# Convolution filters made in pieces inside the first feed-forward stage, their spectra kept in HBM and loaded into x's place; feed-forward blocks of 6, 6, 5 and 5 tiles

## The reference, cut to what matters

```python
def encoder_layer(x, lp):
    x = x + 0.5 * swiglu(rms_norm(x, lp['norm_ffn1']), lp['ffn1_w_in'], lp['ffn1_w_out'])
    h = rms_norm(x, lp['norm_mix'])
    pa, pb, pc = jnp.split(h @ lp['w_in'], [A_COLS, A_COLS + B_COLS], axis=-1)
    ya = rwkv7_mixer(pa, lp)
    yb = group_rms_norm(neighbourhood_attention(pb, lp['na_rpb']), lp['na_out_norm'], B_HEADS)
    yc = group_rms_norm(hyena_mixer(pc, lp), lp['hy_out_norm'], C_GROUPS)
    x = x + jnp.concatenate([ya, yb, yc], axis=-1) @ lp['w_out']
    return x + 0.5 * swiglu(rms_norm(x, lp['norm_ffn2']), lp['ffn2_w_in'], lp['ffn2_w_out'])

def hyena_filters(seq_len, lp):          # from weights and positions alone, never from x
    h = jnp.sin(freq * (z @ w1 + b1)); h = jnp.sin(freq * (h @ w2 + b2))
    h = (h @ w3).reshape(seq_len, 2, HY_ORDER, C_DIM) * jnp.exp(-t * jnp.abs(deltas))
    kern = concatenate([h_fwd, zeros, flip(h_bwd[1:])])
    return kern / jnp.sum(jnp.abs(kern), axis=0)

def hyena_mixer(p, lp):
    v, x1, x2 = jnp.split(short_conv(p), 3, axis=-1)
    kern_fft = jnp.fft.rfft(hyena_filters(seq_len, lp), axis=0)
    z = x1 * (fft_long_conv(v, kern_fft[:, 0]) + v * d_skip[0])
    return x2 * (fft_long_conv(z, kern_fft[:, 1]) + z * d_skip[1])
```

## Time and profile before

| what | value |
|---|---|
| median of 3 runs | 3818.8 us (3816.16 to 3823.51) |
| the profiled execution's own time | 3818.56 us |
| its span | 3816.8 us |
| PE busy | 3555.1 us (93%) |
| PEld busy | 3311.8 us (87%) |
| DVE busy | 1745.3 us (46%) |
| ACT busy | 951.7 us (25%) |
| POOL busy | 33.9 us (1%) |
| chain that ended last, share of PE | 88% |
| mean granted TensorE clock | 0.966 of full |

### The profile page before, as it was taken

How to read it: one execution, slowest core, us unless ns; L and a number is a source line. 1 busy time by engine, 2 the same in 40 slices (tenths; PEclk the granted TensorE clock), 3 DMA queues, 4 the chain that set the end, 5 groups by cost and what they waited for, 6 DMA issues and landing times.

```text
span 3816.8 us, 59772 instructions
## 1 busy us (share of the span) xinstructions
PE 3555.1 (93%) x26416; PEld 3311.8 (87%) x26416; DVE 1745.3 (46%) x2916; ACT 951.7 (25%) x1479; POOL 33.9 (1%) x32
## 2 busy tenths in 40 slices
PE   7999999999858799999999999999998668999997
PEld 7999998878734699999999999988886348999997
DVE  4333346536565543333443333464466564433333
ACT  3212132223251322121321121311233413212121
POOL 0000000000000000000000000000000010000000
PEclk9999999999977899999999999999998789999999
DMA  3111212310230112211112211223004101211211
GB/s 113 64 65 61 66 56 98 107 48 3 84 149 0 39 61 67 70 62 61 61 63 65 67 61 60 96 68 120 16 3 167 66 1 56 67 61 61 67 63 54
DMA packets 67841, 249.67 MB, mean 65 GB/s; under 512 B 7424, under 2 KB 7424, under 8 KB 66176
## 3 DMA queue, kind: packets, MB, share of 16 engines
q1 hardware_dynamic: 67584, 245.85, 19.2%
HBM read 222.23 MB, written 23.59 MB: 64 GB/s over the span
## 4 chain that ended last, share of the span: by engine, by line
PE 88%; DVE 7%; ACT 2%; issue 1%; DMA 1%; POOL 0%; SPq 0%; DVEq 0%; POOLq 0%; ACTq 0%
PE ps L635 87%; DVE uv L1951 1%; PE ps L1067 1%; DVE rstd L1523 0%; DMA hdecay<-hyc 0%; ACT sqb L1167 0%; DMA x<-xT 0%; PE ps L988 0%; DVE hl L1531 0%; DVE NR L1693 0%; DVE sc L2002 0%; ACT sqb L1171 0%; DVE mixed L1882 0%; DVE yab L1959 0%; DVE ml L2027 0%
## 5 line engine op out<-in xcount | busy, mean ns | idle before, releaser
L635 PE MATMUL ps<-hh,wh 128*128 128x384 f32 (+2 forms) x3520 | 1181.2, 336 | 24.6 <-DVE wl L1513 23.6
L635 PE MATMUL ps<-hl,wh 128*128 128x384 f32 (+2 forms) x3520 | 1178.4, 335 | 0.0
L635 PE MATMUL ps<-hh,wl 128*128 128x384 f32 (+2 forms) x3520 | 1177.9, 335 | 0.0
L635 PEld LDWEIGHTS ps<-hh,wh 128*128 128x128 f32 x3520 | 662.8, 188 | 41.2 <-issue 24.2
L635 PEld LDWEIGHTS ps<-hl,wh 128*128 128x128 f32 x3520 | 662.7, 188 | 14.6
L635 PEld LDWEIGHTS ps<-hh,wl 128*128 128x128 f32 x3520 | 662.6, 188 | 14.1
L1190 ACT CAST wh<-wring 128x1024 fp32r<-128x1024 f32 (+1 forms) x340 | 339.7, 1026 | 658.1 <-PE ps L635 653.3
L635 PE MATMUL ps<-act_high,wl 128*128 128x384 f32 x1408 | 470.3, 334 | 0.0
L635 PE MATMUL ps<-act_high,wh 128*128 128x384 f32 x1408 | 470.3, 334 | 0.0
L635 PE MATMUL ps<-act_low,wh 128*128 128x384 f32 x1408 | 470.3, 334 | 0.0
L1574 DVE TENSOR_TENSOR silu<-ps,rstd 128x384 f32<-128x384 f32 x176 | 98.1, 557 | 730.1 <-PE ps L635 730.1
(11 more groups left out here) (260 smaller groups left out, 3440.2 us busy)
## 6 DMA issues: line engine op xcount, KB each, us to landing
wring<-wa SPq DMA_DIRECT2D x308, 512.0 KB, 3.6
wring<-wa SPq DMA_DIRECT2D x32, 384.0 KB, 3.1
bias<-bias SPq DMA_DIRECT2D x24, 512.0 KB, 7.9
conv_q_k<-stage SPq DMA_DIRECT2D x28, 384.0 KB, 2.6
outT<-x SPq DMA_DIRECT2D x2, 3072.0 KB, 9.8
x<-outT SPq DMA_DIRECT2D x2, 3072.0 KB, 25.8
conv<-conv_q_k SPq DMA_DIRECT2D x2, 2304.0 KB, 20.6
vwin<-v_rows SPq DMA_DIRECT2D x14, 256.0 KB, 13.7
```

Source lines behind the costliest of these rows:

```text
L635: return pe.matmul(out, lhsT, rhs, start=start, stop=stop)
```

## The change

`FF_BLOCKS` becomes 6, 6, 5 and 5 tiles, in both feed-forward stages, which frees room behind the activations for the filters' buffers. `filters` leaves the mixer. In the first feed-forward stage each engine calls a `filters` of its own after each unit, and the table `FILTER_AT` says which units are followed by a job: 2 for the network, 6 for taps (two tiles of positions each, one order, 256 columns for each direction), 4 sums, 6 folds. GpSimd adds the magnitudes into `acc` before TensorE sums them over the partitions; the norm is now applied to the spectrum itself, in `kst`, which GpSimd stores to HBM (`kern_rows`), six pieces of 512 KB a layer. GpSimd also loads the filters' inputs and tables. In the mixer SP loads the whole spectrum into x's place and x after the last product of the second convolution; `ftab` and `gtab` are loaded behind bias 4. The transposes of the convolution alternate with the four group norms; v and x1 are copied together, even tiles by VectorE, odd ones by ScalarE.

```diff
-FF_BLOCKS = [(0, 8), (8, 8), (16, 6)]
+FF_BLOCKS = [(0, 6), (6, 6), (12, 5), (17, 5)]
+FF_MOST = max(n for _, n in FF_BLOCKS)
+FF_OUTS = 2 * OUT_TILES * len(FF_BLOCKS)
...
+TAP_TILES = [(0, 1, 2, 3), (4, 5)]
+SEG_FOLDS = [(0, 1), (2,)]
+TAP_GROUPS = [(0, 0), (1, 0), (0, 1), (1, 1)]
+KERNEL_STORES = [(o, a) for o, s in TAP_GROUPS for a in SEG_FOLDS[s]]
+FILTER_AT = {2: ("mlp", 1), 5: ("mlp", 2), 7: ("taps", 0, 0, 0), 8: ("taps", 0, 0, 2), 9: ("sum", 0, 0),
+             13: ("kern", 0, 0), 14: ("kern", 0, 1), 15: ("taps", 1, 0, 0), 16: ("taps", 1, 0, 2), 18: ("sum", 1, 0),
+             20: ("kern", 1, 0), 21: ("kern", 1, 1), 25: ("taps", 0, 1, 4), 27: ("sum", 0, 1), 29: ("kern", 0, 2),
+             35: ("taps", 1, 1, 4), 37: ("sum", 1, 1), 39: ("kern", 1, 2)}
+FILTER_LAST_IN = [("nrm", 0, 0), ("kern", 1, 1), ("kern", 0, 2), ("kern", 1, 2)]
...
+        sums = hy1("sums", [P, 3, 2, 512])
+        odd = hy1("odd", [P, 2, 512])
+        kern = nc.alloc_sbuf_tensor_at("kern", [P, 3, 2, 2, 512], F32, offset=16544)
...
                 sp.dma_start(conv[:, :, :], cqk[l, 0:C_TILES].rearrange("n p t -> p n t")).then_inc(s_cl, 16)
-                sp.wait_ge(s_spill, 16 * (l + 1))
-                sp.dma_start(x[:, :, :], outT).then_inc(s_back, 16)
+                sp.wait_ge(s_kst, 96 * (l + 1))
+                sp.dma_start(kern[:, :, :, :, :].rearrange("p a k t c -> p a (k t c)"),
+                             kern_d[l].rearrange("a p k c -> p a (k c)")).then_inc(s_kl, 16)
+                sp.wait_ge(*rv.at(l, "done", 1))
                 for k in range(BIASES, QUADS):
                     load_bias(k)
-                sp.wait_ge(s_g4, 6 * l + 4)
...
+                    if k == BIASES:
+                        for t, n in ((ftab[:, :, :, :].rearrange("p a b c -> p (a b c)"), "forward"),
+                                     (gtab[:, :, :].rearrange("p a b -> p (a b)"), "inverse")):
+                            sp.dma_start(t, hy_d[:, HOFF[n]:HOFF[n] + dict(HCOLS)[n]]).then_inc(s_hy, 16)
+                sp.wait_ge(s_spill, 16 * (l + 1))
+                sp.wait_ge(*hv.at(l, "dft", 1, FOLD_ORDER[-1]))
+                sp.dma_start(x[:, :, :], outT).then_inc(s_back, 16)
...
+            def filter_taps(l, n):
+                o, s = TAP_GROUPS[n]
+                for p in TAP_TILES[s]:
+                    pool.wait_ge(*fa.at(l, "abs", o, p))
+                    if p == TAP_TILES[s][0]:
...
+                        m = pool.tensor_copy(acc[:, :], taps[:, p % 2, :])
+                    else:
+                        pool.wait_ge(*fg.at(l, "acc", o, p - 1))
+                        m = pool.tensor_tensor(acc[:, :], acc[:, :], taps[:, p % 2, :], ALU.add)
+                    m.then_inc(*fg.inc(l, "acc", o, p))
...
+            def store_kernel(l, n):
+                o, s = TAP_GROUPS[n]
+                for a in SEG_FOLDS[s]:
+                    pool.wait_ge(*fv.at(l, "scaled", o, a))
+                    pool.dma_start(kern_d[l, a][:, :, 256 * o:256 * o + 256], kst[:, :, :]).then_inc(s_kst, 16)
...
+                pool.wait_ge(s_gu, 4 * l * FT + 1)
+                pool.dma_start(w12[0:64, :], hw_d[l, 0:64, 0:HWOFF["w3"]]).then_inc(s_hz, 16)
...
+                load_decay(0)
+                load_table(0)
+                for n in range(len(TAP_GROUPS)):
+                    filter_taps(l, n)
+                    store_kernel(l, n)
+                    if n == 1:
+                        pool.wait_ge(*fv.at(l, "eo", 1, 3))
+                        load_decay(1)
+                        pool.wait_ge(*fp.at(l, "kern", 1, 0))
+                        load_table(2)
...
+            def filters(l, unit, block):
...
+                if block:
+                    pe.wait_ge(s_xup, x_count(l, 0) + 16 * block)
+                if job[0] == "mlp":
...
+                elif job[0] == "taps":
+                    _, o, s, p0 = job
+                    pe.wait_ge(*fa.at(l, "sin", 2))
...
+                    for p in (p0, p0 + 1):
+                        for dr in range(2):
+                            lo = 512 * dr + 256 * o
+                            m = mm(ps[:, 4 + p % 2, 256 * dr:256 * dr + 256], h1[0:64, fold_tokens(p)], hwt[0:64, lo:lo + 256])
+                        m.then_inc(*fp.inc(l, "taps", o, p))
+                elif job[0] == "sum":
+                    _, o, s = job
+                    pe.wait_ge(*fg.at(l, "acc", o, TAP_TILES[s][-1]))
...
+                    for dr in range(2):
+                        m = mm(bank(6, 256), cs("ones"), acc[:, 256 * dr:256 * dr + 256], dr == 0, dr == 1)
+                    m.then_inc(*fp.inc(l, "sum", o, s))
+                else:
+                    _, o, a = job
+                    s, even, odd_ = FOLDS[a]
+                    loads = {0: (2 * l + 1), 1: (2 * l + 1 + o), 2: (2 * l + 2)}[a]
+                    pe.wait_ge(s_tab[a % 2], 16 * loads)
+                    pe.wait_ge(*fv.at(l, "eo", o, TAP_TILES[s][-1]))
+                    if a == 1:
+                        pe.wait_ge(*fv.at(l, "kern", o, 0))
+                    for b, tiles in ((4, even), (5, odd_)):
+                        for trig, src in enumerate((se, so)):
+                            last = (b, trig) == (4, 0)
+                            for g in tiles:
+                                i = g - TAP_TILES[s][0]
+                                m = mm(ps[:, b, 256 * trig:256 * trig + 256], tables[a % 2][:, trig, i, :], src[:, i, :],
+                                       g == tiles[0], g == tiles[-1] and not last)
+                            if last:
+                                pe.wait_ge(*fv.at(l, "skip", o, s))
+                                m = mm(bank(4, 256), cs("ones", SKIP_ROW, SKIP_ROW + 1), skip_sum[SKIP_ROW:SKIP_ROW + 1, 0:256],
+                                       False, True)
+                    m.then_inc(*fp.inc(l, "kern", o, a))
...
+                            if f == 0:
+                                filters(l, 2 * j + hf_, b)
+                    if f == 0:
+                        pe.wait_ge(*fv.at(l, *FILTER_LAST_IN[b]))
...
             def hyena(l):
                 for g in range(6):
                     if g >= 2:
-                        pe.wait_ge(*hv.at(l, "tr", g - 2))
+                        pe.wait_ge(*(ha if g % 2 else hv).at(l, "tr", g - 2))
                     for j in range(4):
                         m = pe.transpose(ps[:, 4 + g % 2, P * j:P * j + P], conv[:, j, fold_tokens(g)], cs("ident"))
                     m.then_inc(*hp.inc(l, "tr", g))
...
+                    if g >= 2:
+                        gnorm()
                 for o in range(2):
                     if o == 0:
-                        pe.wait_ge(*hv.at(l, "tr", 5))
-                    src = vt if o == 0 else zt
+                        pe.wait_ge(*hv.at(l, "tr", 4))
+                        pe.wait_ge(*ha.at(l, "tr", 5))
+                        pe.wait_ge(s_hy, 32 * (l + 1))
+                        pe.wait_ge(s_g3, 6 * l + 4)
+                    src = (lambda g: vx[:, g, 0, :]) if o == 0 else (lambda g: zt[:, g, :])
...
+            def hyena(l):
+                for g in range(6):
+                    if g >= 2:
+                        gn(g)
+                    if g % 2:
+                        sa.wait_ge(*hp.at(l, "tr", g))
+                        sa.copy(vx[:, g, :, :].rearrange("p a c -> p (a c)"), bank(5)).then_inc(*ha.inc(l, "tr", g))
+                    if g >= 3:
+                        gn_root(6 * l + g - 3)
+                gn_root(6 * l + 3)
...
+                if job and job[0] == "taps":
+                    _, o, s, p0 = job
...
+                    for p in (p0, p0 + 1):
+                        ve.wait_ge(*fp.at(l, "taps", o, p))
+                        if p - 2 >= g0:
+                            ve.wait_ge(*fg.at(l, "acc", o, p - 2))
+                        elif (o, s) != TAP_GROUPS[0]:
+                            po, ps_ = TAP_GROUPS[TAP_GROUPS.index((o, s)) - 1]
+                            ve.wait_ge(*fg.at(l, "acc", po, TAP_TILES[ps_][-1]))
+                        by = dec[:, p - g0, :].unsqueeze(1).broadcast_to([P, 2, 256])
+                        m = TT(taps[:, p % 2, :].rearrange("p (d c) -> p d c", d=2),
+                               bank(4 + p % 2).rearrange("p (d c) -> p d c", d=2), by, M)
...
+                        m.then_inc(*fv.inc(l, "win", o, p))
+                        ve.wait_ge(*fv.at(l, "win", o, p))
+                        tf, tb = taps[:, p % 2, 0:256], taps[:, p % 2, 256:512]
+                        TT(se[:, p - g0, :], tf, tb, AD)
+                        TT(so[:, p - g0, :], tf, tb, SU).then_inc(*fv.inc(l, "eo", o, p))
+                if job and job[0] == "sum":
+                    _, o, s = job
...
+                    ve.wait_ge(*fp.at(l, "sum", o, s))
+                    TT(skip_sum[row, 0:256], ps[row, 6, 0:256], hwt[row, sk:sk + 256], M).then_inc(*fv.inc(l, "skip", o, s))
```

(23 more changed lines are left out.)

## The result

The changed kernel takes 3731.5 us (median of 4 runs, 3727.5 to 3735.0) where the kernel before takes 3817.5 in the same comparison (3816.2 to 3823.5): a ratio of 0.977, with a 95% interval of 0.976 to 0.978. The profiled execution took 3734.6 us for a span of 3732.8, 84.0 us less than the span of before. The forecast was 3753 in a range of 3732 to 3784.

The account below looks back on a forecast made before the run. TensorE was taken to bound the kernel, with the first feed-forward stage full. 175.7 us removed, less 104.2 added there, 2 x 1.0 for bias and 2 x 2.0 for clock, gave 65.5: 3818.6 to 3753 us, range 3732 to 3784.

Parts of the forecast that it names:

- the price of a change of shape: First feed-forward stage, TensorE: 1.04 us for going between 128 and 64 rows and back; all shape changes 16.0 a layer.
- the term of 12.6 us for taps, network and skip: First feed-forward stage, per layer: row changes cost 8.3 us for eight network and taps jobs, 4.3 for six folds' skip matmuls.
- The 0.34 us for plain f32 without a change of rows: First feed-forward stage: loss for each of ten sums and folds inside the split stream, 3.4 us a layer.
- The columns' 36.1 us: First feed-forward stage: time of the filter matmuls themselves on TensorE per layer, all at full clock.
- Rival A: First feed-forward stage: shape changes cost 6.1 us for 16.0 a layer, no clock loss or late bias; 3727 to 3742; chance 0.18.
- The stretch that is emptied: Attention's end to the first transform: 18.9 us left where 106.8 and 106.7 stood, 175.7 us removed.
- Bias 5: Attention: the transform tables ahead of it in SP's queue make it late, 1.0 us a layer, range 0 to 1.7.
- The clock of the convolution: First convolution's transforms: part may run at 1.2 GHz after the thinly filled stretch, 2.0 us a layer.
- rival B: First feed-forward stage: eighteen filter jobs a layer wait on chains over four engines; 3766 to 3790 us; chance 0.25.
- The tightest cover: Sum behind unit 9: GpSimd's last magnitudes some 8.2 us after unit 8's end, TensorE arrives 10.9 us after it.
- rival C: First feed-forward stage: VectorE stuck behind GpSimd's stores, slower than before; 3846 us if stores last 40 us; chance 0.03.
- The kernel's and the tables' arrival (D): First transform: held by late arrival of the kernel or tables, so the stretch is not freed; chance under 1 in 50.

Follow-up runs that it names:

- slow_sums: Changed kernel with GpSimd copying the added magnitudes onto themselves eight times more before TensorE sums them; 3744.1 us in one run.
- fill_norms: Changed kernel with unread 512-column matmuls on TensorE, two each ahead of the last two norms among the transposes and of the first transform; 3731.3 us.
- taps_rows: Changed kernel with tap matmuls over 128 rows, 64 of them zeros, instead of over 64; 3732.7 us, first feed-forward stage 599.2 us for 601.7.
- three_edits: Changed kernel with taps over 128 rows, the skip term added without its one-row matmul, and transform tables behind the last bias; 3708.8 us.
- changed_again: The changed kernel unedited, run again as yardstick beside the combined edits; 3734.1 us, ratio 0.978 to the kernel before.

## Why the prediction was wrong in size

**The step that failed is the price of a change of shape**, "0.95 us apart instead of 0.43, 0.52 lost, so 1.04 for going in and out" from the earlier trace rows. The rows are right and the reading is wrong. They are starts of weight loads. In an unbroken stream a load runs ahead of its matmul; at a change of rows this lead is given up, so the first load of the new shape starts later by the lead and by the loss, and the second one takes the lead back (two loads in 0.31 us in the earlier trace rows). Only the loss delays the stream. For the taps I charged the lead as lost twice, going in and going out, and for the skip term once. The matmuls' own rows tell it, in the trace of the kernel before, in the very stretch from which I took the loads (timeline of PE):

```profile
1167.47 1.99 PE L635 MATMUL ps<-hwt,h 64*128 64x512 f32 x4
1169.39 1.13 PE L635 MATMUL ps<-af,cst 128*128 128x512 f32 x2
1170.35 1.02 PE L635 MATMUL ps<-ab,cst 128*128 128x512 f32 x2
1171.30 1.99 PE L635 MATMUL ps<-hwt,h 64*128 64x512 f32 x4
```

One round, in and out, lasts 1171.30 - 1167.47 = 3.83 us; eight records of 512 columns at 0.43 are 3.43. So 0.40 is lost for going in and out, the number that the experiments gave, and it stood in the profile. The lead can be seen in the changed kernel too: ahead of the taps job the last load starts at 98.00 us and its matmul at 98.17, while the first load of the job starts together with its matmul (timeline of PEld; its PE rows stand above):

```profile
98.00 0.19 PEld L729 LDWEIGHTS ps<-hh,wl 128*128 128x128 f32 x1
98.44 1.60 PEld L729 LDWEIGHTS ps<-hwt,h 64*128 64x128 f32 x8 [0.25 <-issue]
```

The loads are 0.44 us apart there, and the matmuls 0.27 for 0.17. The Trainium skill, page "TensorE: Matmul & The Clock Gate", section "Step-by-step: what each phase is for", says that TensorE pulls a weight load ahead of running matmuls, if their row groups don't conflict or it goes to the background buffer; the loads' start ahead of their matmuls in an unbroken stream agrees with that, and why the lead goes at a change from 128 rows to 64 or 1 no run here tells. Per layer the term of 12.6 us for taps, network and skip (8.3 and 4.3) measured 5.6.

**The 0.34 us for plain f32 without a change of rows** (ten jobs, 3.4 us a layer) measured 0.01 a job. In the earlier trace rows the loss sits ahead of the norm's first record: 1365.88 - 1365.47 = 0.41 for 0.17. The weight loads of the same place, in the kernel before, name what it waited for:

```profile
1365.87 0.94 PEld L635 LDWEIGHTS ps<-rstd,cst 128*128 128x128 f32 x4 [0.39 <-DVE rstd L1523]
```

It was a wait for VectorE's operand of the norm, and I had charged it to the format. At the end of the changed kernel's first stage the same records start 0.23 us behind the record in front, the step of their 512-column neighbours, so nothing is lost:

```profile
625.04 1.45 PE L729 MATMUL ps<-rstd,cst 128*128 128x384 f32 x4
```

**The columns' 36.1 us** hold: 41.7 less the 5.6 lost.

**Rival A** was right that the changes cost little, and its sign, a stage longer by 45 us or less, is what came (42.0). The argument that weighed against it, "those rows are the very shapes", was the error above: the right shapes on the wrong engine's row. But its size is in part luck. Its 6.1 us a layer are 0.34 for each of 18 jobs, and the 5.6 measured are 0.41 for twelve, 0.35 for two and next to nothing for four. Its reason, that the matmul before the change is short, doesn't hold: behind records of 0.43 us in the kernel before, a round loses the same 0.40. And it put the late bias and the clock at nothing, where attention grew by 4.4 us and the convolutions by 3.2.

**The stretch that is emptied** was laid out at 18.9 us and took 17.9, or 17.0 where the clock stayed up for most of it: 1.0 us a layer less in the changed kernel's profile.

**Bias 5** was put at 1.0 us a layer and took 3.6 and 0.8. The delay from the tables was near the estimate (15.3 - 8.4 = 6.9 us for 6.4) and VectorE's wait 2.3 us for 1.3. What I left out is the clock: behind the wait TensorE was at the lower level for 3.4 us in layer 0, 1.7 us of work late (4.0 us with the wait, where attention grew by 3.6), the same that slow_sums shows larger; in layer 1 it was not, and the wait of 0.8 us cost 0.8. A wait ahead of TensorE has two prices, and the sum had one. The two layers of this profile are also on the low side: in the eight traces that keep the tables ahead of bias 5, attention took 55.4 to 60.0 us, 3.4 over before's 54.6 on average, so the term was too small by more than half.

**The clock of the convolution** was put at 2.0 us a layer and took 0.2 and 3.0. Before the change, too, its level varied between the layers (82.6 and 80.1 us). The mechanism is right, as fill_norms shows; its size differs from run to run.

**No job waits (rival B)** held: no wait of TensorE in the stage. The tightest cover is smaller than I had it, 1.4 us (last magnitude 117.9, sum 119.3) for 2.7, and it is the one that slow_sums ends. **VectorE and GpSimd's stores (rival C)**: VectorE's waits in the first feed-forward stage name no store. The page of the changed kernel has their time:

```profile
kern_rows<-kst POOLq DMA_DIRECT2D x12, 512.0 KB, 4.1
```

4.1 us (3.3 to 4.5 for the twelve stores) lie between the 2.6 and 8.4 of the earlier trace rows, far from the 35 at which the change would have lost. By the rule of the Trainium skill, page "DMA: Bandwidth & Descriptors", section "Anatomy of one DMA — SWDGE (gpsimd) path", that the prediction cites, the estimate is 3.2 us; the trace's median is 0.9 above it. **The kernel's and the tables' arrival (D)** held nothing: the first transform waits for ScalarE's root, as the row at 1166.10 says, and no engine waits for x behind the convolutions (it landed 10.1 us after its issue, for 8). The second feed-forward stage is unchanged within 0.1 us in four blocks.

## What to carry to other kernels

Price a break in TensorE's stream by the starts of the matmuls, not by a single step between weight loads, and check the price on a whole round in and out: rows of the same shapes give the wrong number when they are another engine's. A small job put into this full TensorE stream cost its columns and 0.2 us for each change of the number of rows, so padding the contraction with zero rows to the neighbours' 128 was cheaper than multiplying over fewer. Count a stop of TensorE twice, once for its length and once for the half clock behind it, and move whatever isn't needed soon behind the transfer that is.

## What the runs showed that I had not expected

- Twice the rows and the same columns made the stage 2.4 us shorter a layer (taps_rows).
- A stop of TensorE of 4.7 us in a stage otherwise without any cost 7.3 and 6.4 us (slow_sums); a wait of VectorE of 2.3 us for a bias made attention 3.6 us longer.
- Matmuls that nobody reads made the two convolutions 2 to 5 us shorter each (78.1 us, for 81.6 and 80.2 in three_edits, 82.9 and 83.1 in changed_again), and the kernel 8 us faster by its median.
- A bias of 512 KB behind 3 MB and 2.6 MB took 15.3 us to land, 6.9 more than behind the 3 MB alone.
